# Eight weight blocks in the ring in place of six, in a fused encoder layer on one core

## The reference

```python
h = h + 0.5 * _swiglu(_rms_norm(h, ffn1_norm), w_gate, w_up, w_down)   # D_FF = 2816
u = _rms_norm(h, mix_norm); proj = u @ w_in                             # pooling mixer, S5 scan, gates
h = h + merged @ w_mix_out
h = h + _cross_attention(_rms_norm(h, xattn_norm), _rms_norm(mem, mem_norm), w_q, w_kv, w_xo)
h = h + 0.5 * _swiglu(_rms_norm(h, ffn2_norm), w_gate, w_up, w_down)
return _rms_norm(h, final_norm)

def _swiglu(u, w_gate, w_up, w_down):
    return (jax.nn.silu(u @ w_gate) * (u @ w_up)) @ w_down
```

## Time and profile before

| | us |
|---|---|
| median of 3 runs | 2041.23 |
| lowest | 2040.27 |
| the profiled execution, its own time | 2042.66 |
| its span, first to last instruction | 2040.9 |

### The profile page before, as it was taken

One profiled execution on the slowest core, in us unless ns is written; L12 is line 12 of the kernel. 1 busy time (PEld: TensorE's weight loads), 2 busy tenths in 40 slices (PEclk: granted clock), 3 DMA queues, 4 the chain that ended last, 5 costly groups with the idle time before them and its releaser, 6 DMA issues.

```text
span 2040.9 us, 24598 instructions
## 1 busy us (share of the span) xinstructions
PE 2017.8 (99%) x9222; PEld 1657.8 (81%) x9222; DVE 1400.5 (69%) x1610; ACT 652.3 (32%) x994; POOL 1202.6 (59%) x803
## 2 busy tenths in 40 slices
PE   9999999999999999999999999999999999999998
PEld 5888888888888888888888888887788888888886
DVE  7778768756876979653252455447876776788687
ACT  5423322333444411002130223335223223244454
POOL 6498888786645533222324421236899988866453
PEclk9999999999999999999999999999999999999999
DMA  7423342447976462422113241311232242288764
GB/s 278 157 93 131 122 142 93 154 142 288 316 241 211 135 172 86 124 84 67 52 35 141 91 137 42 116 40 62 78 134 98 78 134 98 78 297 290 228 202 144
DMA packets 141078, 286.39 MB, mean 140 GB/s; under 512 B 12832, under 2 KB 38048, under 8 KB 140576
## 3 DMA queue, kind: packets, MB, share of 16 engines
q1 hardware_dynamic: 100528, 232.68, 33.9%
q10 hardware_dynamic: 40432, 52.13, 7.8%
HBM read 222.39 MB, written 63.42 MB: 140 GB/s over the span
## 4 chain that ended last, share of the span: by engine, by line
PE 87%; DVE 8%; issue 2%; ACT 2%; POOL 1%; POOLq 0%; DVEq 0%; ACTq 0%
PE ps L546 86%; DVE w_lo L2512 1%; DVE h L2521 1%; DVE xt_lo L2502 1%; DVE ua_lo L1937 1%; DVE xb_lo L2246 0%; DVE acc L1928 0%; DVE h L2280 0%; POOL w_lo L1197 0%; DVE xt_lo L2222 0%; ACT xb_hi L1485 0%; POOL h L1370 0%; POOL raw L1222 0%; ACT prob L1379 0%; DVE ua_lo L1928 0%
## 5 line engine op out<-in xcount | busy, mean ns | idle before, releaser
L1197 POOL TENSOR_TENSOR w_lo<-raw,w_hi 128x512 fp32r<-128x512 f32 x352 | 543.2, 1556 | 199.0 <-ACT w_hi L1437 198.0
L546 PE MATMUL ps<-xt_hi,w_hi 128*128 128x512 f32 x1320 | 515.7, 391 | 3.6 <-DVE acc L2251 1.9
L546 PE MATMUL ps<-xt_hi,w_lo 128*128 128x512 f32 x1320 | 514.4, 390 | 0.0
L546 PE MATMUL ps<-xt_lo,w_hi 128*128 128x512 f32 x1320 | 514.1, 389 | 0.0
L1437 ACT ACTIVATE w_hi<-raw 128x512 fp32r<-128x512 f32 x462 | 284.8, 625 | 464.5 <-PE ps L546 318.4
L1212 POOL TENSOR_SCALAR w_hi<-raw 128x1024 fp32r<-128x1024 f32 x53 | 63.0, 1188 | 454.3 <-PE ps L546 376.9
L546 PEld LDWEIGHTS ps<-xt_hi,w_hi 128*128 128x128 f32 x1320 | 248.2, 188 | 58.0 <-DVE acc L2251 2.3
L546 PEld LDWEIGHTS ps<-xt_hi,w_lo 128*128 128x128 f32 x1320 | 248.0, 188 | 51.9
L546 PEld LDWEIGHTS ps<-xt_lo,w_hi 128*128 128x128 f32 x1320 | 248.2, 188 | 51.2
L1222 POOL TENSOR_TENSOR raw<-raw 128x512 f32<-128x512 f32 x177 | 263.4, 1499 | 17.0 <-DMA raw<-in_gu 9.8
L546 PE MATMUL ps<-ua_hi,w_hi 128*128 128x512 f32 x608 | 237.3, 390 | 0.8 <-DVE ua_lo L1937 0.8
(11 more groups left out here) (322 smaller groups left out, 2843.7 us busy)
## 6 DMA issues: line engine op xcount, KB each, us to landing
raw<-in_dn SPq DMA_DIRECT2D x264, 256.0 KB, 3.5
raw<-in_gu SPq DMA_DIRECT2D x88, 512.0 KB, 4.9
raw<-in_weights SPq DMA_DIRECT2D x54, 512.0 KB, 3.5
d_act<-f_g SPq DMA_DIRECT2D x20, 512.0 KB, 2.8
d_act<-acc SPq DMA_DIRECT2D x20, 512.0 KB, 2.8
d_act<-sq SPq DMA_DIRECT2D x20, 512.0 KB, 4.2
xt_hi<-d_act SPq DMA_DIRECT2D x20, 512.0 KB, 5.5
xt_lo<-d_act SPq DMA_DIRECT2D x20, 512.0 KB, 4.9
```

The costliest lines, as they stand in the source:

```text
L546: ins = nc.tensor.matmul(out, lhsT, rhs, start=start, stop=stop)
L1197: add(lo, src, hi.bitcast(F32), op=ALU.subtract).then_inc(s_w_low["pool"], 1)
```

## The change

`RING` becomes 8. The two tensors grow by two places each, 8192 bytes per partition together, which are taken from the scratch that the program sets aside for dynamic DMAs (from its default to 8192 bytes). In its loops ACT writes the high half of the block eight steps on. The two more blocks that are needed at the start of each feed-forward layer stand in its opening. Nothing else is moved: the four raw buffers, DVE's `w_low(f, d + 2)`, `act_high(f, d + 4)` and SP's order are as they were. PE's order of instructions is the same in both.

```diff
-RING = 6
+RING = 8
@@ ScalarE, second feed-forward layer's opening
                     for k in range(KP):
                         block(k, 2)
+                    for op in ops[7:RING]:
+                        block_high(op)
                     act.wait_ge(s_xt_lo, 2 * KP * (f + 1))
@@ ScalarE, gate and up
-                        if f == 0 or j:
-                            block_high(ops[j + 6])
+                        block_high(ops[j + RING])
                         if n == FT - 1 and i >= 3:
                             act_high(f, i - 3)
@@ ScalarE, down
                 for d in range(DN_N):
                     if d + 4 < DN_N:
                         act_high(f, d + 4)
-                    if GU_N + d + 6 < len(ops):
-                        block_high(ops[GU_N + d + 6])
+                    if GU_N + d + RING < len(ops):
+                        block_high(ops[GU_N + d + RING])
@@ ScalarE
-            ffn(0, 0, {("b", 0): slice(0, 2), ("b", 1): slice(2, 4), ("b", 2): slice(4, 6)}, beside_gate_up, ua_hi)
+            ffn(0, 0, {("b", 0): slice(0, 2), ("b", 1): slice(2, 4), ("b", 2): slice(4, 7)}, beside_gate_up, ua_hi)
@@ kernel
-    nc = bacc.Bacc("TRN2", target_bir_lowering=False, num_devices=1)
+    nc = bacc.Bacc("TRN2", target_bir_lowering=False, num_devices=1,
+                    dynamic_dma_scratch_size=8192)
```

## The result

The changed kernel takes 2067.22 us in the median (2064.94 to 2070.88, four runs) against 2040.75 us before: ratio 1.0129, with a 95% interval of 1.0117 to 1.0141. It is 26 us slower, which is inside the range and under 2%; the forecast was +18.9 us.

The account below looks back on a forecast made before the run. PE was taken to bound the kernel, busy 2017.8 of 2040.9 us with its clock granted in full. Terms -2.3 + 3.6 + 16.6 + 1 = +18.9 us on the median of 2041.2 gave 2060 us, range 2040 to 2085.

Parts of the forecast that it names:

- last products: Last two products of down: the loop's lateness mostly covered by slack, +1 us for both layers (0 to 10.6).
- Part 1: Second layer's opening: ACT's earlier high halves let POOL fill its gap and end PE's wait, a gain of 2.3 us.
- If that cover is gone, the price is 1.6 + 0.6 us: Both openings: ACT's added waits fall into its gaps and cost nothing; otherwise one POOL sum and one write.
- Part 2: Seam from gate and up to down: step 2's activations wait behind step 6's late high half, +3.6 us for two.
- step 3 may feel: Seam: DVE's delayed work may also hold up step 3; only the upper bound was raised, to 2.2 us.
- Part 3: Down phase: ACT feeds itself through DVE, DMA and POOL over three turns; +16.6 us products 1 to 3, +1 last.
- 9.3, as in the passage: 0.38 a step: Down phase: one passage of the chain takes 9.3 us, 1.14 too long for three PE steps, 0.38 a step.
- some 4 us late: Start of down: ACT begins turn 5 near 519.4 us in place of 514.9, leaving 2.7 us of 6.7 slack.
- The rival of the hidden loop: Down phase: chain of 8.2 us or shorter costs nothing; 2042.5 us, within 2038 to 2046, chance 0.19.
- Part 4: Halved scratch for dynamic DMAs costs nothing, since nothing uses it; moved tensors also costed at nothing.
- The signs named ahead: Down-phase gaps ended by `xt_lo`, ACT idle for POOL's sum, one gap per seam, POOL's 6.09 us idle gone.
- the sign of being wrong: Wrong if PE's down phases stay at 2.72 us a step, waits fall on another engine, or gate and up lengthens.

Follow-up runs that it names:

- E4: Changed kernel, ACT copies the first finished bank of the second layer's first product in turn 1 in place of 3: 2067.88 us, ratio 1.0129.
- E8: Changed kernel, but ACT stays six blocks ahead, in the old order, for the second layer's first 14 steps: 2062.11 us, ratio 1.011.
- E13: Changed kernel, eight ahead, with bank copies, table load, norm and gate activations two turns earlier on ACT in the second layer's opening: 2063.56 us, ratio 1.0111.
- E6: Changed kernel, ACT writes activations ahead of the weight's high half in the last seven turns of gate and up: 2063.11 us, ratio 1.0109.
- E3: Changed kernel, DVE writes the low half of a summed down-phase block four steps ahead in place of two: 2053.36 us, ratio 1.0059.
- E5: Changed kernel, ACT seven blocks ahead in the down phase, seam included, in place of eight: 2047.21 us, ratio 1.0028.
- E9: Changed kernel, DVE writes the low half of a summed down-phase block one step ahead in place of two: 2171.91 us, ratio 1.0641.
- E1: Kernel before the change, with only the scratch for dynamic DMAs cut to 8192 bytes: 2042.54 us, ratio 1.0005.
- E11: Changed kernel, down phase loads only 64 of 512 columns of each pair's second block (output differs): 2054.21 us, ratio 1.0065.
- E12: Changed kernel, POOL's down-phase sums cover 256 of 512 columns (output differs): 2052.72 us, ratio 1.0057.
- E10: Changed kernel with the edits of E3, E6 and E8 together: 2040.07 us against 2040.47, ratio 0.9997.

## Why the prediction came out as it did

**The class and the range were right, the sum partly by luck.** Forecast +18.9, measured +24.0 us of span. By terms: opening -2.3 against +4.9; seams +3.6 against +6.6; products 1 to 3 +16.6 against +10.2; last products +1 against +2.3 (3.0 with steps 72 to 76); scratch 0 against 0. Two errors of 7 and 6 us with opposite signs nearly cancel; the difference that is left comes from the seams and the last products.

**Part 1 had the wrong sign; this is the step that failed.** It said that POOL's 2.3 us would be won because its high half "stands behind a bank copy on ACT; two blocks of it now go ahead". It looked at what moves ahead and not at what it moves ahead of. The blocks that pass the copy are summed ones, which wait for POOL. The copy, the table load, the norm and the gate's activations each came to stand behind two more of POOL's sums. E4 shows that curing the first alone isn't enough, E8 and E13 that the order is all of it. Nor was there a gain to have: with the order cured, in E13, PE still waits 1.5 us for POOL and 1.3 for ACT there. POOL's low half there waits for two sums of POOL's own, and no lead of ACT changes that (argued from POOL's order, not tested). "If that cover is gone, the price is 1.6 + 0.6 us" was too little as well, since a delay there meets a chain without slack, and it had no term for the clock, which took 1.7 us more. (The 9 of a slice in the earlier trace rows says 90% or more and not "in full": before the change, too, the clock was at its lower level for 3.4 us at 77.8 us.)

**Part 2 had the mechanism and the first gap (1.83 us, taken as 1.8, though "the row's own duration" is 1.66 and its sum gives 1.9 with it).** The term was mis-sized because "step 3 may feel" it was left out of the value: it felt 0.93. Each gap also costs PE some 0.25 us more than the wait itself. 3.3 us a seam lie above the bound of 2.2. E6 shows the cause.

**Part 3 had the place, the engine, the chain and its length; its size was off by what it took for ACT's lateness at the start.** E3 and E5 confirm the chain (three turns lose, four don't). The term "9.3, as in the passage: 0.38 a step" held: the changed kernel's 29 turns show 9.24 and 9.05 us, or 0.36 and 0.30 us a turn. What failed is "some 4 us late": ACT wrote the high half of turn 4 as soon as the activations before it were done, since POOL had summed that block in time, and began turn 6 only 1.6 us late in the first layer and 0.4 in the second:

```profile
513.86 1.33 POOL L1277 TENSOR_TENSOR raw<-raw 128x512 f32<-128x512 f32 x1 [0.37 <-DMA raw<-in_dn]
...
515.44 0.62 ACT L1437 ACTIVATE w_hi<-raw 128x512 fp32r<-128x512 f32 x1
```

The forecast took this sum's start, 517.22 us, from a kernel in which ACT and POOL were two blocks further back: POOL ended its last low half of product 0 at 514.80 us there and at 511.79 here. By terms, a layer was to lose 4.0 + 11.0 - 6.7 = 8.3 us, and it lost 1.6 + 10.4 - 5.4 = 6.6 and 0.4 + 8.6 - 5.5 = 3.5. (5.4 and 5.5, what PE let pass of ACT's lateness, are by difference; the 6.7 counted DVE's low half at its shortest.) So two wrong terms hid each other here as well. The constant rate didn't show in PE: its gaps came in 9 and 4 steps of 29, from 0.1 to 1.6 us each, and products 1 to 3 lost from 3.2 to 6.6 us in layer 1 by kernel.

The rival of the hidden loop, with 8.2 us, was wrong at three turns. Its argument that "a slower pace would spread them out" has something in it: E9's two turns average 8.3 and 8.0 us, and 7.46 in the passage shown, where the same 9.3 had made me expect 170 to 190 us in place of 105. The Trainium skill's estimate for the pair (page "DMA: Bandwidth & Descriptors", section "Anatomy of one DMA", which states it for transfers that GpSimd issues, where here SP does) gave 7.2 us for the chain; E9's 7.46 is close to it, and the changed kernel's 9.2 is not.

**Part 4 was right** (E1). The signs named ahead were seen: gaps ended by `xt_lo`, ACT idle for POOL's sum. A seam showed two gaps, not one, and "gate and up gets longer" was the sign of being wrong that came true.

**Left open:** how much of the 9.2 us of a passage is DMA traffic and how much the meeting of POOL and DVE (E11 and E12 each removed the whole loss), and what makes the gaps in the last steps of the second down phase so uneven with the same order.

## What to carry to other kernels

In programs of fixed order, writing further ahead doesn't add slack; it moves a wait ahead of everything that stood between. List what each moved step passes, and ask of each what it was just in time for. If the ring gets deeper and the buffers that feed it don't, count the turns that the chain through those buffers spans: here a chain of some 9 us lost nothing over four steps (10.9 us), 12 us in the whole kernel over three (8.16 us), and 109 over two (5.44 us), though it had shortened to 8 us by then. When you price a gap of PE, add what the clock may take after it. Before paying for depth, check which wait it would end: this kernel had 2.7 us to win there, and E10, with all cures and eight places, won none of it.

## What the runs showed of the hardware

- Two of PE's gaps at the seam, with waits of 1.83 and 0.93 us, made the matmuls start 1.99 and 1.09 us late, and the matmul after each started 0.31 us behind the one before in place of 0.23. Some 0.25 us come on top of each wait, of which 0.16 is that the profile lets a matmul end 0.39 us after its start while the next one starts 0.23 us after it.
- VectorE's operations on 128 by 8 numbers take 0.17 us while POOL is idle (E13, from 1428.6 to 1429.18 us), and 1.15 to 1.22 us beside POOL's operations of 1.29 us (after, from 1433.86 to 1438.76). A reciprocal (0.20 us) and an operation that reads a bank of PE (0.17) weren't held up beside them. The Trainium skill (page "SBUF — State Buffer", section "SBUF: two separate sides") states a lock for a whole instruction; the trace agrees, and it shows that a chain of tiny operations suffers most, 1 us for each link.
- Loads of 256 KB landed in 3.8, 3.4, 2.9 and 2.6 us in the median (before, after, E9, E11), with 280, 243, 203 and 183 GB/s moved in the same stretches (515 to 605 us, in E9 1898 to 1990).
- In E9's first down phase PE was busy 79% of the stretch, and the granted clock was 0.91 in the mean, since it was at the lower level (1.2 GHz) in four pieces of 3.4 or 6.8 us and at the upper (2.4 GHz) otherwise. Before and after the change it is 1.00 there:

```profile
545.00:662.00 117.00, 91.97 (x348) 70.48 (x349) 64.93 (x77) 35.62 (x63) 39.84 (x30) 0.91 0.56 184
```
- Around PE's gap of 3.7 us in the second layer's opening the clock fell to the lower level for 3.4 us (after) or 6.8 us (E4), and right after gaps of 2.1 and 2.2 us in the last products for 3.4 us (E6, E13). The gap of 2.3 us at 1443.45 us in the changed kernel was followed by no fall, nor were those of 1.6 us and less in the same places (before, E8, E10). With PE busy throughout, 3.4 us at the lower level cost 1.7 us.
